# Fillings of a delta-rule inverse on one Trainium2 core: two steps fewer at two points of a pair, one step more at four

## What is computed

```python
def step(state, inp):
    r_t, w_t, k_t, v_t, a_t, b_t = inp
    sa = jnp.einsum("bhij,bhj->bhi", state, a_t)
    state = (state * w_t[:, :, None, :] + sa[..., None] * b_t[:, :, None, :]
             + v_t[..., None] * k_t[:, :, None, :])
    return state, jnp.einsum("bhij,bhj->bhi", state, r_t)
...
proj = h @ w_in
p_r, p_m, p_d, p_g = jnp.split(proj, _split_points([RWKV_COLS, MAMBA_COLS, DIFF_COLS, GATE_COLS]), axis=-1)
```

## Time and profile before

| | |
|---|---|
| time, median of 3 runs | 2776.01 us (2775.69 to 2776.02) |
| profiled execution, its time | 2780.25 us |
| its span, first to last instruction | 2778.5 us |
| TensorE busy | 2688.9 us, 97% of the span |
| VectorE busy | 1412.2 us, 51% |
| ScalarE, GpSimd busy | 487.5 us, 231.1 us |
| chain that ended last, by engine | PE 81%, DVE 7%, DMA 7% |
| mean granted TensorE clock | 0.991 |

### The profile page before, as it was taken

One profiled execution on the slowest core, in us unless ns is written; L12 is line 12 of the kernel. 1 busy time (PEld: TensorE's weight loads), 2 busy tenths in 40 slices (PEclk: granted clock), 3 DMA queues, 4 the chain that ended last, 5 costly groups with the idle time before them and its releaser, 6 DMA issues.

```text
span 2778.5 us, 55843 instructions
## 1 busy us (share of the span) xinstructions
PE 2688.9 (97%) x24765; PEld 1955.3 (70%) x24765; DVE 1412.2 (51%) x2558; ACT 487.5 (18%) x1012; POOL 231.1 (8%) x372
## 2 busy tenths in 40 slices
PE   7999999999999999999999999999999999999999
PEld 6667977777876455477787678778778755546776
DVE  3552346776774866313035522567767758562001
ACT  1000122212121332100010011222212123321000
POOL 6000101100001101010000001020000011100000
PEclk9999999999999999999999999999999999999999
DMA  9884432322235543384569834332232265324442
GB/s 359 314 321 156 140 116 88 122 81 81 89 111 187 187 164 114 126 308 137 169 232 334 287 122 145 133 105 73 89 99 96 90 230 190 141 103 165 136 160 98
DMA packets 226305, 444.43 MB, mean 160 GB/s; under 512 B 7544, under 2 KB 102326, under 8 KB 226064
## 3 DMA queue, kind: packets, MB, share of 16 engines
q1 hardware_dynamic: 211376, 395.59, 40.9%
q0 software_dynamic: 12960, 38.98, 4.4%
q10 hardware_dynamic: 1728, 6.29, 0.6%
HBM read 422.88 MB, written 17.96 MB: 159 GB/s over the span
## 4 chain that ended last, share of the span: by engine, by line
PE 81%; DVE 7%; DMA 7%; issue 1%; ACT 1%; POOL 1%; SPq 0%; DVEq 0%; ACTq 0%; POOLq 0%
PE ps L1018 79%; DMA ring<-in_ffn_w 4%; DVE scratch L2174 3%; DVE scratch L2177 1%; DMA ring<-in_w_in 1%; DVE merged L2458 1%; DMA scratch<-fill_scratch 1%; DVE scratch L2180 1%; PE ps L1047 1%; DMA scratch<-in_ada_w 1%; DMA scratch<-acs_scratch 0%; DMA acs_scratch<-scratch 0%; ACT scratch L2146 0%; POOL scratch L977 0%; PE ps L1645 0%
## 5 line engine op out<-in xcount | busy, mean ns | idle before, releaser
L1018 PE MATMUL ps<-hT,ring 128*128 128x256 f32 (+1 forms) x5824 | 1148.6, 354 | 14.7 <-ACT hT L1806 5.6
L1018 PEld LDWEIGHTS ps<-hT,ring 128*128 128x128 f32 x5824 | 965.6, 191 | 152.1 <-issue 23.3
L1018 PE MATMUL ps<-scratch 64*64 64x32 f32 (+7 forms) x15136 | 851.7, 256 | 24.6 <-issue 5.6
L1018 PEld LDWEIGHTS ps<-scratch 64*64 64x64 f32 (+4 forms) x15136 | 571.2, 141 | 334.2 <-issue 225.8
L2174 DVE TENSOR_TENSOR scratch<-scratch,ps 128x256 f32<-128x256 f32 (+3 forms) x314 | 155.2, 494 | 689.9 <-ACT scratch L1860 551.6
L1018 PE MATMUL ps<-ring,hT 128*128 128x256 f32 (+1 forms) x1280 | 422.0, 476 | 2.1 <-DMA ring<-in_w_in 2.1
L1018 PEld LDWEIGHTS ps<-ring,hT 128*128 128x128 f32 x1280 | 237.0, 192 | 137.3 <-issue 112.5
L2174 DVE TENSOR_TENSOR scratch<-scratch 128x512 f32<-128x512 f32 (+4 forms) x426 | 278.2, 653 | 52.1 <-ACTq L1983 12.8
L1018 PE MATMUL ps<-ring,scratch 128*128 128x512 f32 x512 | 234.7, 593 | 0.5
L2180 DVE SCALAR_TENSOR_TENSOR scratch<-scratch,ccol 128x1024 f32<-128x1024 f32 x120 | 154.2, 1285 | 6.4 <-DMA scratch<-in_ada_w 2.1
L1860 ACT ACTIVATE scratch<-ps 128x512 f32<-128x512 f32 x40 | 23.9, 597 | 749.6 <-PE ps L1018 749.6
(11 more groups left out here) (223 smaller groups left out, 1389.3 us busy)
## 6 DMA issues: line engine op xcount, KB each, us to landing
ring<-in_w_in SPq DMA_DIRECT2D x56, 2048.0 KB, 8.5
ring<-in_ffn_w SPq DMA_DIRECT2D x88, 1024.0 KB, 10.1
scratch<-in_ada_w SPq DMA_DIRECT2D x35, 2048.0 KB, 14.3
scratch<-in_ffn_w SPq DMA_DIRECT2D x44, 1024.0 KB, 5.0
ring<-in_w_branch_mamba SPq DMA_DIRECT2D x8, 2048.0 KB, 7.9
scratch<-acs_scratch POOLq DMA_DIRECT2D x24, 512.0 KB, 6.3
scratch<-fill_scratch SPq DMA_DIRECT2D x16, 512.0 KB, 9.3
ring<-in_w_branch_rwkv SPq DMA_DIRECT2D x4, 2048.0 KB, 11.1
```

The costliest lines, as they stand in the source:

```text
L1018: return pe.matmul(o, lhsT, rhs, start=start, stop=stop)
```

## The change

```diff
-FILL_PAIR = (("ops", 12), ("mid", 8), ("lv", 8), ("k0", 2), ("k1", 2), ("k2", 2), ("k3", 2),
+FILL_PAIR = (("ops", 12), ("mid", 6), ("lv", 6), ("k0", 3), ("k1", 3), ("k2", 3), ("k3", 3),
...
                     if q:
-                        fill_evacuations(q - 1, "lv")
+                        fill_evacuations(q - 1, "k3")
                         if q - 1 in CONV_SIGMOID:
                             conv_sigmoid(CONV_SIGMOID[q - 1])
...
                     else:
-                        fill_evacuations(p, "lv")
+                        fill_evacuations(p, "k3")
                         conv_sigmoid(CONVS - 1)
```

## The result

The changed kernel is slower: 2801.73 us (median of 5 runs, 2792.57 to 2810.65) against 2775.69 us (5 runs, 2773.34 to 2776.02), ratio 1.0101, 95% interval 1.0077 to 1.0124. I had forecast 2791 us and 2781 to 2799, so the sign and the mechanisms were right and the time lies above my range. Two later measurements gave 1.0063 [1.0041, 1.0085] and 1.0064 [1.0045, 1.0083], that is 2794.49 and 2796.68 us. Most of what follows is about why the number is 18 us and was once 26.

The account below looks back on a forecast made before the run. TensorE, busy 2688.9 of 2778.5 us, was taken as the bound, so only waits could change. Terms 8.0 + 0.9 + 3.4 + 2.6 = 14.9 us gave 2790.9 us against the median of 2776.0; predicted 2791, range 2781 to 2799.

Parts of the forecast that it names:

- `mid`, 8.9 us: Between the directions: two steps less cover make TensorE wait for VectorE's mask, 8.0 us in pairs 2 to 7, 0.9 in pair 0.
- `lv`, 0: In front of the levels: 0.9 us to spare against 0.86 taken away, priced at 0, at worst 1.6 us.
- the levels, 0: In the levels: a third step in each filling covers no wait, so 0 gained.
- Pair 1, 3.4 us: Pair 1, level 0: unit 9 ends later, so ScalarE, VectorE's taps and `dd` run late; TensorE waits 1.7 us per layer.
- ScalarE's order, 0: Pairs 2, 3 and 5: units of the levels go ahead of the sigmoid; 0 us, up to 10.7 if cover were gone.
- The clock behind pair 1, 2.6 us: After pair 1's wait in each layer the granted clock falls to 1.2 GHz, costing 1.3 us each time.
- rival (b): Same waits, but layer 0's pauses and long slow stretch go: +5.3 to +10 us, 2781 to 2786 us; chance 0.22.
- What I cannot price: TensorE pauses from late instruction blocks and half clock behind them: -9.6 us to a similar amount above, taken as 0.

Follow-up runs that it names:

- The dose: Changed kernel with 4 steps at `mid` instead of 6 and 8 at `lv`, levels at 3 as in the change: 2807.50 us against 2778.10 before, ratio 1.0105.
- the kernel with `mid` kept: Against the kernel before: `mid` stays 8, `lv` 6, levels 0 to 2 get 3 steps, level 3 one, ScalarE's new order: 2779.23 us against 2779.34, ratio 0.9993.
- light loads: Kernel before, with the fillings' weight loads cut to 64 of 512 columns: 2767.00 us against 2776.45, ratio 0.9966.

## Why the prediction was right or wrong

**`mid`, 8.9 us.** The mechanism was right and the term too small: 11.3 us. I took the pick-up after VectorE as 0.02 us, from the first `dd` of a pair of two; behind the mask it is 0.12 (562.46 to 562.58). With 0.10 more in each place, 12 x 0.77 + 2 x 0.56 = 10.4. And in pair 1 the spare time of 1.08 us did not last: its products of direction 1 wait 0.4 us in layer 0 and 0.6 in layer 1. In the kernel before, the filling there took 4.39 us and not 3.72, since it began in the half-clock stretch of the earlier trace rows: 0.67 of the 1.08 us that I read as spare were slow clock, not cover. In the second measurement's trace the clock did not fall ahead of it, and there pair 1 waits 0.89 us in both layers. The dose confirms the size of a step, 0.43 us.

**`lv`, 0, and the levels, 0.** Right: the 0.33 us stands in every such place of both kernels, and the kernel with `mid` kept takes the time of before (0.9993).

**Pair 1, 3.4 us.** Right in its chain, ScalarE, the ninth tap, `dd`, and slightly small: 2.06 - 0.26 = 1.80 us in each layer, 3.6 in all, which is the whole of ScalarE's work on the unit, my upper bound.

**ScalarE's order, 0.** Right: 0.9988 for that part alone.

**The clock behind pair 1, 2.6 us.** Right in kind. I expected a fall behind the wait in each layer. In the six profiled executions that have the wait, one followed in one of the two layers and never in both: 10.2 us long in the first, 6.8 us in two and 3.4 us in three. By my own price, half of the stretch, that is 5.1 us once and 1.7 to 3.4 otherwise. The Trainium skill ("TensorE: Matmul & The Clock Gate", section "Why this matters for your kernels") warns only of longer idle gaps, by which I had 12.3 us for the sum; the rows of six executions speak against it here, where the work around the gap is small matmuls. What I did not see is that the clock part of the whole kernel is no sum of such prices, since stretches elsewhere come and go with it. The long stretch of layer 0, which rival (b) expected to go, is missing in all three full-load traces of the changed kernel, and yet its clock part in the second and third measurements is that of before.

**The sum, and the step that failed.** With 11.3 in place of 8.9 and 3.6 in place of 3.4 my sum is 17.5 us, and the second and third measurements have 18.4 and 18.0 by means. The first has 26.0. The step that failed is the term "What I cannot price", the loss to pauses and clock, which I took as 0: in the first measurement it was 8.5 us, the 26.0 less the 17.5. The undersized waits of `mid` and pair 1 are 2.6 us of the error; with them right the forecast would have been 2793.5 us, still 8 below the measured time. In those five executions the granted clock was 0.985 to 0.992, and the clock part 29.7 us, against 19.6 and 21.9 in the two later measurements of the same kernel, while the rest is 2771.6, 2775.5 and 2774.0 us. The mean time was 6.2 and 5.3 us longer than in the later two, and even six tenths of the difference in the clock part are 6.1 and 4.7 us. So by the granted clock the time beyond my range was lost clock, which the same kernel did not show again; where it was lost is not shown, since only the fastest of the five left a trace. In the two later measurements the same term was near 0 (18.4 and 18.0 against 17.5), so on which side of 2799 the time fell was the draw of the measurement.

The pauses put down to issue moved, as I had expected of them, but their sum hardly changed: 5.6 us before, 6.1, 8.3 and 6.6 in three executions of the changed kernel. Whether late blocks of instructions made them is shown in part: light loads took away three fifths of them, and two pauses are left. The Trainium skill ("Runtime: NRT & Kernel Launch", section "Instruction fetch mechanics") calls that crossing mostly hidden. If the pauses are such crossings, the traces agree with "mostly": there are 194 blocks in the kernel and six to eight pauses in the pairs. But they are not free, at 0.35 to 1.9 us each, and their sum is not fixed for certain: it was 0.5, 2.7 and 1.0 us above before in those three executions.

What stays open is why the clock falls in one execution and not in the next at the same instruction. The wait of pair 1 was followed by a fall in layer 0, in layer 1, or for longer, in traces that agree in this wait; nothing that I read in them tells those cases apart.

## What to carry to other kernels

Before cover is moved from one place to another, measure the spare time at each: at the place that gives, the arrival against the end of what is waited for, with the pick-up of that very wait, and at full clock; at the place that gets, whether the pause in the profile has a releaser that is really late. Here `mid` had 0.1 us to give (0.21 less a pick-up of 0.12) and gave 0.86, and none of the places that got had a wait. Look at which unit of a stream ends where: a unit that slides behind one group of matmuls put three engines in a row, 1.8 us in each layer. And a gap that looks fixed (2.0 us ahead of pair 1) was the better target: filling it gave 0.2% (0.02 to 0.33). A half-clock stretch followed that gap in 17 of the 24 places where it stands in twelve traces, and none in the kernel that fills it. But the mean clock part of that kernel is only 0.3 us lower, so what is shown of the gain is the wait and not the clock.

## What the runs showed that I had not expected

- The kernel before took 2771 to 2788 us in 35 executions on one chip. The longer ones have the lower clock, with a correlation of -0.74. Differences below 5 us could be read only from the waits in the traces, or after the split by clock.
- A pause "issue" of 0.33 us on the weight loads absorbs nothing: it grows to 1.10 and 1.97 us when VectorE is late and still has that name. The row of the matmul names VectorE.
- A pause put down to issue costs up to 2.1 us at once; in the kernel with `mid` kept one stood in the middle of a group of 64x32 matmuls:

```profile
733.53 1.64 PE L1018 MATMUL ps<-scratch 64*64 64x32 f32 x43 [2.08 <-issue]
```
